# Opening of a two-layer transformer kernel in four feature groups, with later sums over w_ada on ScalarE and GpSimd

## The reference, cut to what matters

```python
def hybrid_layer(x, c, positions, norm_g, w_ada, b_ada, w_in, ...):
    mod = jax.nn.silu(c) @ w_ada + b_ada                 # c is 1 x 1024, w_ada 1024 x 3072
    shift, scale, gate = jnp.split(mod[:, None, :], 3, axis=-1)
    h = rms_norm(x, norm_g) * (1 + scale) + shift        # x is 256 x 1024
    z = h @ w_in
    c_q, c_kv, k_rope, g_mla, q_b, k_b, v_b, g_moba = jnp.split(z, list(IN_OFFSETS), axis=-1)
    o_mla = mla_attention(c_q, c_kv, k_rope, ...)
    o_moba = moba_attention(q_b, k_b, v_b, ...)
    y = jnp.concatenate([silu(g_mla) * o_mla, silu(g_moba) * o_moba], axis=-1) @ w_out
    return x + gate * y
```

## Time and profile before

| | us |
|---|---|
| median of 3 runs | 1597.88 (1596.69 to 1599.29) |
| the profiled execution, its own time | 1596.89 |
| its span | 1594.7 |
| TensorE busy in the span | 1552.5 |
| VectorE, ScalarE, GpSimd busy | 1069.9, 869.8, 117.0 |

### The profile page before, as it was taken

How to read it: one execution, slowest core, us unless ns; L and a number is a source line. 1 busy time by engine, 2 the same in 40 slices (tenths; PEclk the granted TensorE clock), 3 DMA queues, 4 the chain that set the end, 5 groups by cost and what they waited for, 6 DMA issues and landing times.

```text
span 1594.7 us, 21371 instructions
## 1 busy us (share of the span) xinstructions
PE 1552.5 (97%) x7540; PEld 1290.8 (81%) x7540; DVE 1069.9 (67%) x1789; ACT 869.8 (55%) x1534; POOL 117.0 (7%) x142
## 2 busy tenths in 40 slices
PE   4989999999999999999999999999999999999998
PEld 4777887788888888888888888888888888888886
DVE  7987877666555766787756557565666578766553
ACT  3676667455445656565644446444566666554442
POOL 0310021011000000021000001000000002100000
PEclk9999999999999999999999999999999999999999
DMA  9964673379854634546565557975463444665651
GB/s 340 322 233 158 196 239 128 104 180 221 222 185 158 198 96 133 174 141 213 197 200 170 198 184 197 199 205 192 158 199 118 139 160 147 211 207 172 205 184 71
DMA packets 149026, 293.03 MB, mean 184 GB/s; under 512 B 10096, under 2 KB 23184, under 8 KB 148920
## 3 DMA queue, kind: packets, MB, share of 16 engines
q1 hardware_dynamic: 143424, 276.60, 51.5%
q0 software_dynamic: 4352, 12.15, 6.2%
q10 hardware_dynamic: 1144, 2.92, 0.5%
HBM read 290.57 MB, written 1.06 MB: 183 GB/s over the span
## 4 chain that ended last, share of the span: by engine, by line
PE 88%; DVE 5%; ACT 3%; issue 2%; DMA 1%; POOL 0%; DVEq 0%; SPq 0%; ACTq 0%
PE pb L475 83%; PE pb L479 5%; DMA raw<-in_w_ada 1%; DVE wl L1529 1%; ACT wh L906 1%; ACT pb L906 1%; DVE mkv L1526 1%; POOL st L2461 0%; DMA raw<-in_w_in 0%; DVE qt L1526 0%; ACT xt_h L906 0%; DVE mk L1529 0%; ACT mkv L906 0%; DVE B L1529 0%; DVE pb L1532 0%
## 5 line engine op out<-in xcount | busy, mean ns | idle before, releaser
L906 ACT ACTIVATE wh<-raw 128x1024 fp32r<-128x1024 f32 (+1 forms) x484 | 506.5, 1053 | 424.6 <-PE pb L475 394.2
L1529 DVE TENSOR_TENSOR wl<-raw,wh 128x1024 fp32r<-128x1024 f32 (+1 forms) x484 | 581.4, 1218 | 197.6 <-ACT wh L906 193.6
L475 PE MATMUL pb<-wh,xt_h 128*128 128x512 f32 (+2 forms) x1472 | 578.1, 393 | 4.0 <-ACT xt_h L906 2.5
L475 PE MATMUL pb<-wh,xt_l 128*128 128x512 f32 (+2 forms) x1472 | 572.4, 389 | 1.4 <-DVE xt_l L1529 1.0
L475 PE MATMUL pb<-wl,xt_h 128*128 128x512 f32 (+2 forms) x1472 | 569.6, 387 | 0.0
L475 PEld LDWEIGHTS pb<-wh,xt_l 128*128 128x128 f32 x1472 | 277.1, 188 | 64.1 <-DVE xt_l L1526 5.9
L475 PEld LDWEIGHTS pb<-wh,xt_h 128*128 128x128 f32 x1472 | 277.2, 188 | 59.5 <-issue 4.0
L475 PEld LDWEIGHTS pb<-wl,xt_h 128*128 128x128 f32 x1472 | 277.4, 188 | 52.5
L475 PE MATMUL pb<-wh,big_h 128*128 128x512 f32 x352 | 137.7, 391 | 0.0
L475 PE MATMUL pb<-wh,big_l 128*128 128x512 f32 x352 | 137.0, 389 | 0.0
L475 PE MATMUL pb<-wl,big_h 128*128 128x512 f32 x352 | 137.0, 389 | 0.0
(11 more groups left out here) (242 smaller groups left out, 1546.5 us busy)
## 6 DMA issues: line engine op xcount, KB each, us to landing
raw<-in_ffn_w_gu SPq DMA_DIRECT2D x160, 512.0 KB, 4.9
raw<-in_w_in SPq DMA_DIRECT2D x148, 512.0 KB, 4.3
raw<-in_ffn_w_down SPq DMA_DIRECT2D x88, 512.0 KB, 3.9
raw<-in_w_ada SPq DMA_DIRECT2D x48, 512.0 KB, 5.3
raw<-in_w_out SPq DMA_DIRECT2D x32, 512.0 KB, 4.1
raw<-in_w_branch SPq DMA_DIRECT2D x24, 512.0 KB, 4.2
raw<-in_ffn_w_gu SPq DMA_DIRECT2D x32, 256.0 KB, 4.9
raw<-in_w_in SPq DMA_DIRECT2D x8, 416.0 KB, 4.8
```

Source lines behind the costliest of these rows:

```text
L475: return e.matmul(o, a, b, start=start, stop=stop)
L906: return e.activation(o, a, func, **kw)
L1529: return e.tensor_tensor(o, a, b, op)
```

## The change

The opening of layer 0 is written out by hand on each engine. The columns of shift and scale of w_ada for 256 features are one group: four chunks of 512 KB hold the 1024 rows of 2 x 256 columns. After the sums of a group, h is made for two row blocks of 128 features, and z, qb and kb are summed together over them in six banks (qb and kb in one chunk of 1024 columns per row block), while VectorE weighs the next group. x is loaded first, by SyncE, and turned before it is scaled and shifted; ScalarE then writes both the rounded and the full affine result. Ten small loads move from ScalarE's to GpSimd's queue. The bias table's addition `mbias`, the transposes and the lower parts of the latents come after vb; the rotary angles come before it; an Exp table load is placed there too.

For the later tiles ScalarE multiplies a row of w_ada by its weight in place (in the raw buffer; the first row of a tile into the accumulator), and GpSimd adds it to the accumulator; the raw buffer is free after that sum. `SUMS` says how many rows GpSimd takes between its other operations. All `later` steps of layer 0 start after vb, `over(16)`.

The diff, cut to its core:

```diff
+    acc_free = {(0, 4): ("modm", 3), (1, 2): ("tr", ("mobak", 0), 2), (1, 4): ("turn", 0, 5)}
     side_tiles = [[(1, 0), (0, 4), (1, 2)], [(1, 4)]]
-    acc_of = {(0, 0): mkv[:, 0, :], (0, 2): mkv[:, 1, :], (0, 4): acc[:, :], (1, 4): acc[:, :],
-              (1, 0): qt[:, 4:8, :].rearrange("p a b -> p (a b)"), (1, 2): qkv[:, 0, 0:DM]}
-    acc_free = {(1, 2): ("tr", ("mobak", 0), 2), (1, 4): ("turn", 0, 5)}
+    x_turned = mkv[:, :, :].rearrange("p a b -> p (a b)").rearrange("p (c n) -> p c n", n=256)
+    group_sums = [acc[:, 512 * i:512 * i + 512] for i in range(2)]
+    SUMS = ((0, 0, 0, 14, 10), (3, 2, 1, 2, 0))
...
+    def read_out(what):
+
+        if what[0] == "first":
+            return ("gsum", what[1], 2 * what[2] + 1)
+        l, j, kx = what
+        return ("accp", l, j, kx) if kx else ("prod", l, j, 0)
...
+        def column_sums(g):
+
+            b = open_bank(4 + g % 2, ("modk", g, 1))
+            w.wait_ge(*at("ones"))
+            w.wait_ge(*at("gsum", g, 7))
+            for f in range(4):
+                last = mm(b[:, f:f + 1], group_sums[g % 2][:, f * 128:f * 128 + 128], ones[:, 0:1], True, True)
+            last.then_inc(*up("modm", g))
...
+            def blocks(g, half):
+                for r in (2 * half, 2 * half + 1):
+                    if len(plan) == c_no[0]:
+                        plan.append((wa[:, 2 * r:2 * r + 2, 0:2, 256 * g:256 * g + 256], 2, 512, None, None, ("first", g, r)))
+                    c_no[0] += 1
+
+            def latents_chunk(kx):
+                return take(wi[:, kx:kx + 2, 0:416], 2, 416, ("mm", ("z", 0), 1) if kx == 6 else None)
+
+            def heads_chunk(kx):
+                return take(wi[:, kx:kx + 1, 928:1952], 1, DM, ("mm", ("kb", 0), 1) if kx == 7 else None)
...
+            for t in range(2):
+                for c0 in (0, 4):
+                    b = open_bank((2 if t else 6) + c0 // 4, ("xevd" if c0 else "xev", t))
+                    w.wait_ge(*at("xnv" if t else "xn", 0, t))
+                    for c in range(c0, c0 + 4):
+                        last = tr(b[:, (c - c0) * 128:(c - c0) * 128 + 128], xn[:, t, c * 128:c * 128 + 128])
+                    last.then_inc(*up("tr", ("x", 0), t, c0))
...
+            keep_busy(5)
+            column_sums(0)
...
+            for kx in range(8):
+                g, odd = kx // 2, kx % 2
+                if not odd:
+                    zc = latents_chunk(kx)
+                qk = heads_chunk(kx)
+                if g < 3:
+                    blocks(g + 1, odd)
+                for t in range(2):
+                    if odd and t and g < 3:
+                        column_sums(g + 1)
+                    xh, xl = (v[:, kx, t * 128:t * 128 + 128] for v in XT)
+                    parts = []
+                    for nm, where, (c, hi, lo), m in (("z", ACC_Z, zc, None), ("qb", ACC_Q, qk, 0), ("kb", ACC_K, qk, 512)):
+                        row, n = (odd, slice(0, 416)) if m is None else (0, slice(m, m + 512))
+                        o = banks[where[t]][:, 0:n.stop - n.start]
+                        parts.append((nm, where[t], c, o, hi[:, row, n], lo[:, row, n]))
+                    w.wait_ge(*at("xh", ("x", 0), kx))
+                    for nm, i, c, o, hi, lo in parts:
+                        if kx == 0:
+                            open_bank(i, ("eva", (nm, 0), t))
+                        w.wait_ge(*at("hi", c))
+                        mm(o, xh, hi, kx == 0, False)
+                    for nm, i, c, o, hi, lo in parts:
+                        w.wait_ge(*at("lo", c))
+                        mm(o, xh, lo, False, False)
+                    w.wait_ge(*at("xl", ("x", 0), kx))
+                    for nm, i, c, o, hi, lo in parts:
+                        last = mm(o, xl, hi, False, kx == 7)
+                        if kx == 7:
+                            last.then_inc(*up("mm", (nm, 0), t))
+                        elif t == 1 and nm == "z" and odd or t == 1 and nm == "kb":
+                            last.then_inc(*up("w", c))
+            pair_no[0] += 2
...
+                later.add(ada(side_tiles[l]), 10 * len(side_tiles[l]))
+                later.over(16)
             turn_heads(("mobaq", l), lambda j, t: qkv[:, t, j * 128:j * 128 + 128], 4, 128,
                        lambda t: [("nrm", "qb", l, t)])
             turn_heads(("mobak", l), lambda j, t: qkv[:, t, 512 + j * 128:512 + j * 128 + 128], 4, 128,
                        lambda t: [("nrm", "kb", l, t)])
+            if l == 0:
+                latents()
...
@@ ScalarE @@
+                    if ada_[0] != "first":
+                        weigh(c)
...
+            w.wait_ge(*at("csil"))
+            if kx == 0 and (l, j) in acc_free:
+                w.wait_ge(*at(*acc_free[l, j]))
+            ac_(v if kx else acc_of[l, j], v, scale=stat(8, "c_silu")[:, kx:kx + 1]).then_inc(*up("prod", l, j, kx))
...
+            split(stream.lead(4))
+            for g in range(4):
+                split(stream.lead(2))
+                w.wait_ge(*at("modk", g, 1))
+                if g == 0:
+                    w.wait_ge(*at("xev", 1))
+                if g == 2:
+                    for t in range(2):
+                        w.wait_ge(*at("xevd", t))
+                for kx in (2 * g, 2 * g + 1):
+                    affine = {"scale": ac[0][:, kx:kx + 1], "bias": mod[:, 0, kx:kx + 1]}
+                    ac_(xt_h[:, kx, :], x_turned[:, kx, :], ACT.Identity, **affine).then_inc(*up("xh", ("x", 0), kx))
+                    if kx >= 2:
+                        w.wait_ge(*at("xl", ("x", 0), kx - 2))
+                    ac_(xtmp[kx % 2], x_turned[:, kx, :], ACT.Identity, **affine).then_inc(*up("xma", ("x", 0), kx))
+                split(stream.lead(5 if g < 3 else 1))
+                if g == 0:
+                    w.wait_ge(*at("relmm"))
+                    ac_(mk[0:8, 0, 0:512], banks[ACC_Z[1]][0:8, :], scale=8.0).then_inc(*up("relb8"))
+                if g == 1:
+                    e.dma_start(cst[:, 128:], d["consts"][:, 128:C_OH]).then_inc(*landed("cst"))
+            split(stream.lead(2))
+            stream.taken = stream.freed = 12
+            pair_no[0] += 2
+            z_, q_, k_ = to(lambda t: z0[:, t, :]), to(lambda t: qkv[:, t, 0:512]), to(lambda t: qkv[:, t, 512:1024])
+            for t in range(2):
+                q_(("qb", 0), t, banks[ACC_Q[t]])
+                squares(("qb", 0, t), qkv[:, t, 0:512], 512, [("eva", ("qb", 0), t)])
+                k_(("kb", 0), t, banks[ACC_K[t]])
+                squares(("kb", 0, t), qkv[:, t, 512:1024], 512, [("eva", ("kb", 0), t)])
+                z_(("z", 0), t, banks[ACC_Z[t]][:, 0:416])
+                split(stream.lead(1))
+            latent_squares(0)
...
@@ VectorE @@
+                    if ada_[0] == "first":
+                        weigh(c)
...
+            for cc in (2 * r, 2 * r + 1):
+                weight = stat(8, "c_silu")[:, cc:cc + 1]
+                if cc == 0:
+                    if g >= 2:
+                        w.wait_ge(*at("modm", g - 2))
+                    ts(a, v[:, cc % 2, :], weight, None, ALU.mult, None).then_inc(*up("gsum", g, cc))
+                    continue
+                w.wait_ge(*at("gsum", g, cc - 1))
+                stt(a, v[:, cc % 2, :], weight, a, ALU.mult, ALU.add).then_inc(*up("gsum", g, cc))
...
+            split(stream.lead(2))
+            for t in range(2):
+                w.wait_ge(*at("rsq", 0, t, 0))
+                ts(stat(1, "rv", 0, t), stat(1, "rn", 0, t, 0), 1.0 / DM, EPS, ALU.mult, ALU.add).then_inc(
+                    *up("var", "rn", 0, t))
+            w.wait_ge(*at("rs", "rn", 0, 1))
+            ts(xn[:, 1, :], h[:, 1, :], stat(1, "rs", "rn", 0, 1), None, ALU.mult, None).then_inc(*up("xnv", 0, 1))
+            split(stream.lead(1))
...
+            for g in range(4):
+                if g:
+                    split(stream.lead(1))
+                modulation(g)
+                split(stream.lead(1 if g else 2))
+                for kx in (2 * g, 2 * g + 1):
+                    w.wait_ge(*at("xh", ("x", 0), kx))
+                    w.wait_ge(*at("xma", ("x", 0), kx))
+                    tt(xt_l[:, kx, :], xtmp[kx % 2], xt_h[:, kx, :].bitcast(F), ALU.subtract).then_inc(
+                        *up("xl", ("x", 0), kx))
+                split(stream.lead(5 if g < 3 else 1))
+            split(stream.lead(2))
...
+            def opening_steps():
+                for t in range(2):
+                    head_scale("qb", 0, (t,))
+                    head_scale("kb", 512, (t,))
+                    yield
...
+                side.add(opening_steps(), 4)
+                side.over(4)
...
@@ GpSimd @@
+        def sums(n):
+
+            for _ in range(n):
+                c, (l, j, kx) = rows_left.popleft()
+                w.wait_ge(*at("prod", l, j, kx))
+                if kx > 1:
+                    w.wait_ge(*at("accp", l, j, kx - 1))
+                if kx:
+                    a = acc_of[l, j]
```

(31 more changed lines are left out.)

424 lines of the change are left out of this document (179 added, 245 removed).

## The result

| | before | after |
|---|---|---|
| median of the runs compared, us | 1598.59 (1596.69 to 1600.66) | 1642.55 (1640.58 to 1643.51) |
| ratio | | 1.0273, 95% interval 1.0255 to 1.0291 |
| the profiled execution, its span | 1596.89, 1594.7 | 1642.27, 1640.5 |

A forecast was written before the change was run, and what follows sets the result against it. TensorE, busy 97%, was taken as the bound. +16.3 at the hand-over, +3 for ScalarE's rows and -1 for VectorE's relief made +18.3, less 1.3 gave +17: 1597.9 to about 1615 us, range 1594 to 1627.

The forecast's parts named there:

- Part 1: Start of layer 0 up to the first product: it would come at about 24.7 us, a gain of 9 us.
- Part 2: The opening's four groups: VectorE's chain sets 11.2 us a group, all three sums ready at 66.8 us, gain left 3 us.
- The rival with half clock: Opening: TensorE drops to half clock, a group takes 17 us instead of 11.2, 11 us in two groups: 1626; chance 0.1.
- Part 3: Turn to vb: TensorE waits 3.0 us in all for z's banks; vb ends at 80.3 us, even with before.
- Part 4, the hand-over: Around vb's end: rows queued on ScalarE and GpSimd delay vb's emptying; q0 starts at about 100.1 us, +16.3.
- rival 4: GpSimd contention at full price: two sums cost 2 us more each, powers of mq and mk 4 late: +25, 1623; chance 0.14.
- Rows 10 to 13 on ScalarE: From q0 to the third step of moba's attention: 3.9 us added to ScalarE's full queue, priced +3 (0 to 4).
- VectorE's relief: Same stretch behind q0: VectorE, freed of the rows, may give back lateness, priced -1 (-3 to 0).
- after that TensorE is the bound again: Behind the third step of moba's attention: TensorE bounds again and ScalarE has room for rows 14 to 18.
- The gate's sum asks for row 16 some 20 us after: nothing: After the mla transposes: the gate's sum needs row 16 some 20 us after GpSimd may add it, no cost.
- Layer 1: Only 8 such rows over 26 chunks, waits and relief together priced 0 (-2 to +2).
- Contention: GpSimd and VectorE both adding from SBUF, the later operation blocked: nothing in the sum, 0 to 5 us in the range.

The follow-up runs named there:

- e1: Changed kernel with all 32 later rows of w_ada weighed by VectorE again, none on ScalarE or GpSimd; four-group opening kept: 1612.9 us, ratio 1.0093.
- e6: Changed kernel with the rows' additions made by VectorE instead of GpSimd; ScalarE's 32 products stay: 1624.1 us.
- e2: Changed kernel with six unread filling products on TensorE ahead of its waits for the group sums of groups 1 to 3: 1643.5 us.
- e3: Changed kernel with GpSimd adding four rows before its wait for mla's transposes instead of behind it: 1637.2 us.
- e4: Changed kernel with only layer 1's 8 later rows weighed by VectorE as before: 1638.3 us.
- e5: Changed kernel with ScalarE holding later rows, and chunks whose buffers depend on them, until vb is emptied and the latents scaled: 1643.3 us.
- e11: Changed kernel with later rows on VectorE and seven of layer 1's eight shift rows left out, neither loaded nor weighed: 1604.8 us.
- e12: e10 plus the filling products ahead of the group sums and z's banks emptied before qb's and kb's: 1617.3 us.
- e8: Kernel before, with its own opening and spreading of rows, but later rows multiplied by ScalarE and added by GpSimd: 1624.6 us.
- e9: Kernel before, rows still on VectorE, but all 24 later rows of layer 0 start after vb, over 16 chunk steps: 1605.3 us, ratio 1.0041.
- e10: Changed kernel with later rows on VectorE, and ScalarE and VectorE holding them back until the latents' upper and lower parts are written: 1617.6 us.

## Why the prediction was wrong in size

The loss as the runs divide it, each term a difference of two medians: opening with its packed rows 14.4 (e1 less before), products on ScalarE 11.1 (e6 less e1), sums on GpSimd 18.5 (after less e6). They make 44.0. Set against the prediction's own terms, the hand-over was nearly right, and what was priced at +2 behind it (+3 and -1) and at nothing for the gate's sum and layer 1 came to +27.4 (13.0, 9.0 and 5.3).

- **Part 1** (first product 24.7): 21.7. The filling products took 2.62 us for ten, not 4.61: sixteen transposes ran right ahead of them and were slow instead (3.67 us, 2.76 before). The column sum took 0.95 us, not 1.8. The granted clock is on record as 1.00 both times, so that no half clock shows in this start. The lead was 12 us, not 9.
- **Part 2** (11.2 a group): right in two of three cycles (11.8, 11.3). The 14.8 was priced nowhere: I had set the loads at 9.2 to 11 us a group and called VectorE's chain the longest, but the ring puts eight chunks of two kinds in one line, and the middle of the opening waits for loads, at full clock too (e2). The rival with half clock was half right: the clock fell twice. The first fall cost nothing that shows: e3, e4, e5 and e11 were no faster without it. For the second no run tells, but TensorE still waited 0.73 us for VectorE's last sum behind it (57.48). The bound of 75 us that I gave for this case does not fit the rival's own 11 us, which make it 78. The last group took 9.8 us from its modulation, not 8.0, for nine products of the group before stand behind the column sums. That the three sums were ready within 1.6 us of the forecast is in part luck: 3.0 us too early at the first product, 4.6 us lost from there on.
- **Part 3** (3.0 us of waiting, even): 0.74 and 2.26, as forecast; what z's banks emptied first would win was not isolated (e12).
- **Part 4, the hand-over** (+16.3): +18.4 at q0, mechanism and times as described, with vb emptied at 97.2 for 95.1: the powers were through 0.7 us later, and one of the two sums took 4.34 us instead of 2.5. That is rival 4's price of 2 us a sum, paid once. What I had not asked is whether the pause was the price. e5 took 13 us of it away and the end did not move, in part because holding rows back costs too.
- **"Rows 10 to 13 on ScalarE" (+3, VectorE's relief -1) and "after that TensorE is the bound again"**: +13.0 from q0 to gmla. This is the step that failed, the term that was mis-sized most. ScalarE multiplied eleven rows between q0 and gmla's first Tanh, about 11.4 us of work at 1.04 from one to the next, and I had priced four and given the others away, though the earlier trace rows had shown ScalarE at 22.0 of 26 us and VectorE at 23.0. TensorE was not the bound again: of the 13.0 us, 6.5 were lost up to mla's first Tanh (102.0 before, 126.9 after), and 6.5 behind it. e6 and e1 differ by the same eleven products, and by 7.9 us in this stretch (48.5 against 40.6), 0.7 us a row. VectorE's relief is inside these differences and did not show by itself: in e8 the rows left VectorE and the kernel lost 26.7.
- **"The gate's sum asks for row 16 some 20 us after: nothing"**: +9.0 from gmla to gmoba. I followed the sum to its reader and not its buffer to the next load. GpSimd's wait for the transposes stood ahead of two sums; e3 moved them and got 5.4 back; in e6, with no sums on GpSimd, 8.6 of the 9.0 are gone.
- **Layer 1** (0, up to 2 either way): +5.3, of which e4 gave back 4.3. Two sums stand ahead of the powers of z. In layer 0 I had asked what stands ahead of what in GpSimd's queue, here I had not.
- **Contention** (0 to 5 us): its rows are there. VectorE's timelines of after, beside GpSimd's sums, and of e1, without them:

```profile
84.52 3.40 DVE L1597 TENSOR_SCALAR z<-z,st 128x256 f32<-128x256 f32 x4
```
```profile
92.06 1.32 DVE L1601 TENSOR_SCALAR z<-z,st 128x256 f32<-128x256 f32 x4
```

The same four scalings of z took 3.40 and 1.32 us; one of them took 2.36 by itself, beside the first sum, and the others 0.28 to 0.35. GpSimd's sums took 2.35 alone, as forecast (2.5), and up to 4.34, the one beside `mbias` above, which cost the hand-over 2 us. The rule of the Trainium skill that I had set beside the earlier trace rows (SBUF — State Buffer, "SBUF: two separate sides": a locked port, the later operation blocks) fits these rows: the operation that came later took some 2 us more, about what the earlier one still had to run. `mbias` has two inputs in SBUF. The scalings read one tensor only, and fit if they count among the operations in a two-port mode that the page names too; no run here tells that. e6 took sums and contention away together, so that its part of the 18.5 us is open.

Of the opening's own 14.4 us, 7 to 8 are, if the parts add, rows that it leaves for the stretch behind vb (e9, e11). The other 6 to 7 are not isolated. What the traces show beside them: an opening that ends 2.7 us later in e1's profiled execution than in after's (vb from 71.8, not 69.1), vb's two waits, the transposes of the latents after vb and no longer under kb, and the clock at 0.67 in 88 to 96 us in e1 (1.00 before), after a pause of 3.1 us. What the half clock cost after behind q0 (0.50 to 0.52 in 120 to 127, 144 to 151 and 168 to 178 us) is inside the parts above and was not isolated either: it follows pauses for ScalarE there.

## What to carry to other kernels

Price a move of work by the stretch that it moves into, and count all of it there: where two engines are some 85% busy between the steps of a chain, an operation added costs much of its duration (0.7 us of 1.04 for a product on ScalarE in e6, 1.16 us for a row with its load in e11). Over the whole kernel less comes through: 32 such products, some 33 us of work, cost 11.1. Follow each operation that frees a buffer to the next load into that buffer, not only its result to its reader; holding work back holds its buffer too (e5, e10). And when a predicted pause appears in the trace as predicted, take it away before you call it the cause, and look at what the taking away costs.

## What the runs showed of the hardware beyond this

GpSimd adds 128 x 1024 numbers from SBUF in 2.35 to 2.38 us and VectorE multiplies and adds as many in 1.28, so handing a row to ScalarE and GpSimd turned 1.28 us into 1.04 + 2.35 on two engines. TensorE's clock fell to half after pauses of 1.7 us and after longer ones, for some 6 to 10 us at a time (0.50 in 32 to 38 and 168 to 178). But the length of a pause alone does not tell: behind a pause of 1.7 us at the same place the clock at 32 to 38 us was 0.50 in after, 0.72 in e10 and 1.00 in e4 and e11, and a pause of 2.26 us inside vb left it at 1.00 (73 to 82). With six filling products per pause it was 1.00 in 22 to 45 us in e2, though 0.73 in 45 to 51 (1.00 there in e12). The DMA engines stood at a share of 1.02 to 1.08 with 365 to 372 GB/s in 38 to 51 us, with w_ada in transfers of 256 KB and w_in in up to 512 KB, and at 1.03 with 408 GB/s in 20 to 30 us of the kernel before, with whole rows. One addition on GpSimd beside a two-input addition on VectorE took 4.34 us for 2.35, and one scaling on VectorE beside a GpSimd addition 2.36 us for 0.35.
